# Three chained transformer blocks on one core: causal masks added by VectorE in PSUM, a last tile of squares that goes straight into the means, an activation table fetched early, and branch outputs rounded in two steps

## The reference, cut to what matters

```python
# block 1: three branches are gated and summed, projected, added; then a norm
y  = gates[0]*y_a + gates[1]*y_b + gates[2]*y_c
h  = x + g1 * (y @ w_out)                      # residual "out1"
h2 = modulate(rms_norm(h, norm2_g), sh2, sc2)  # norm "n2", read by the SwiGLU "ff1"
# block 2: two layers of FFN, attention, FFN; the attention has 8 "fox" and
# 4 "diff" heads (each diff head has two score matrices), causal
s = q @ k.T * scale (+ forget bias);  s = where(k_pos <= q_pos, s, -inf)
p = softmax(s)
# between blocks 2 and 3
x = x + 0.5 * swiglu(...)                      # residual "f2_1"
x = _rmsnorm(x, final_norm)                    # row "fin2"
h = rms_norm_3(x, norm_g) * (1 + scale) + shift  # norm "n3"
# block 3: a linear recurrence beside 8 causal attention heads of width 64
```

## Time and profile before

| | us |
|---|---|
| median of three runs | 3472.44 |
| the profiled execution | 3478.79 |
| its span, first to last instruction | 3477.0 |
| TensorE busy in the span | 3398.7 (98%) |
| VectorE, ScalarE, GpSimd busy | 1234.8, 1249.2, 1475.5 |
| mean granted TensorE clock | 0.989 of full |

### The profile page before, as it was taken

The page is one execution under the profiler, slowest core; times in us unless marked ns, Lnnn a source line. Parts: engine busy times, 40 slices in busy tenths (PEclk is TensorE's granted clock), DMA queues, the critical chain, the costliest instruction groups (busy, mean ns, idle before and its releaser), DMA issues.

```text
span 3477.0 us, 38568 instructions
## 1 busy us (share of the span) xinstructions
PE 3398.7 (98%) x15758; PEld 2725.9 (78%) x15758; DVE 1234.8 (36%) x2140; ACT 1249.2 (36%) x1988; POOL 1475.5 (42%) x674
## 2 busy tenths in 40 slices
PE   8999999998999999999999999999999999999998
PEld 5777788887888888887677888888887778888776
DVE  3266775623221134212553111211123642111554
ACT  4534323533222232223554222322233653222543
POOL 4322445654544444445424444444436234444332
PEclk9999999999999999999999999999999999999999
DMA  7211233442333323434213333333333123333211
GB/s 272 67 55 61 97 97 121 157 140 73 122 127 128 98 96 135 139 97 117 67 34 103 97 96 94 94 99 97 94 104 101 39 76 97 97 95 99 73 61 55
DMA packets 102174, 345.41 MB, mean 99 GB/s; under 512 B 12173, under 2 KB 12557, under 8 KB 101838
## 3 DMA queue, kind: packets, MB, share of 16 engines
q1 hardware_dynamic: 101200, 341.10, 30.9%
q10 hardware_dynamic: 798, 1.85, 0.2%
HBM read 336.08 MB, written 2.10 MB: 97 GB/s over the span
## 4 chain that ended last, share of the span: by engine, by line
PE 89%; DVE 4%; ACT 2%; DMA 2%; POOL 1%; issue 1%; SPq 0%; ACTq 0%; DVEq 0%
PE ps L1201 25%; PE ps L1203 24%; PE ps L1202 24%; PE ps L1232 2%; PE ps L1233 2%; PE ps L1234 2%; PE ps L1502 2%; PE ps L1532 1%; DMA t<-in_w_ada 1%; PE ps L1515 1%; POOL t L2675 1%; DVE t L2105 1%; PE ps L1421 1%; PE ps L1435 0%; ACT t L1893 0%
## 5 line engine op out<-in xcount | busy, mean ns | idle before, releaser
L2675 POOL TENSOR_TENSOR t<-t,t 128x1024 fp32r<-128x1024 f32 (+2 forms) x584 | 1354.4, 2321 | 1886.4 <-ACT t L1590 1882.4
L1201 PE MATMUL ps<-t,t 128*128 128x512 f32 x4016 | 1597.8, 398 | 19.6 <-POOL t L2675 13.7
L1203 PE MATMUL ps<-t,t 128*128 128x512 f32 x4016 | 1573.1, 392 | 0.0
L1202 PE MATMUL ps<-t,t 128*128 128x512 f32 x4016 | 1568.4, 391 | 0.0
L1201 PEld LDWEIGHTS ps<-t,t 128*128 128x128 f32 x4016 | 758.0, 189 | 196.0 <-issue 24.1
L1203 PEld LDWEIGHTS ps<-t,t 128*128 128x128 f32 x4016 | 757.4, 189 | 166.1
L1202 PEld LDWEIGHTS ps<-t,t 128*128 128x128 f32 x4016 | 758.3, 189 | 157.7 <-issue 1.7
L1590 ACT CAST t<-t 128x1024 fp32r<-128x1024 f32 (+2 forms) x588 | 584.1, 995 | 575.1 <-PE ps L1203 414.9
L2454 DVE TENSOR_TENSOR t<-t,ps 128x512 f32<-128x512 f32 x110 | 75.7, 688 | 537.0 <-PE ps L1203 522.4
L1656 ACT CAST t<-t 128x512 fp32r<-128x512 f32 x158 | 97.2, 622 | 408.0 <-DVE t L2454 357.5
L1849 ACT ACTIVATE t<-t 128x512 f32<-128x512 f32 x88 | 55.6, 632 | 311.7 <-DVE t L2447 311.6
(11 more groups left out here) (296 smaller groups left out, 2225.3 us busy)
## 6 DMA issues: line engine op xcount, KB each, us to landing
t<-in_w_f1i SPq DMA_DIRECT2D x88, 512.0 KB, 3.6
t<-in_w_f2i SPq DMA_DIRECT2D x88, 512.0 KB, 3.6
t<-in_w_ada SPq DMA_DIRECT2D x72, 512.0 KB, 4.5
t<-in_w_ffi SPq DMA_DIRECT2D x44, 512.0 KB, 4.1
t<-in_w_f1o SPq DMA_DIRECT2D x32, 512.0 KB, 3.5
t<-in_w_f2o SPq DMA_DIRECT2D x32, 512.0 KB, 3.5
t<-in_w_gate SPq DMA_DIRECT2D x24, 512.0 KB, 4.3
t<-in_w_out SPq DMA_DIRECT2D x48, 256.0 KB, 2.7
```

The lines of the kernel that those rows point to most:

```text
L1201: e.matmul(out, wh[:, at], X.hi[c][:, 0:N], start=c == first, stop=False)
L1202: e.matmul(out, wh[:, at], X.lo[c][:, 0:N], start=False, stop=False)
L1203: m = e.matmul(out, wl[:, at], X.hi[c][:, 0:N], start=False, stop=c == final)
L2675: e.tensor_tensor(k.WL[:, n % NHL, 0:w], k.raw[:, j % NRAW, 0:w], f(k.WH[:, n % NHL, 0:w]), ALU.subtract).then_inc(*k.rest.inc(('rest', j) ...
```

## The change

It has four parts.

1. **Masks.** The two mask matmuls of each job go (160 in all). VectorE adds the causal tile, now fp32 in SBUF, to the last 128 columns of both score matrices in PSUM, then takes the two maxima. The two VectorE copies that had prepared the bf16 tiles go too.
2. **Split sums** ("n2" and "n3" only). The sum in SBUF is finished with the seventh tile. The squares of the eighth aren't added by VectorE: TensorE takes the means of the sum, and adds those of the eighth tile's squares in the same PSUM columns.
3. **Table.** Behind the squares of the seventh tile (n = 6) of "out1" and "f2_1" ScalarE takes the square root of a constant into a spare column, and the table of the roots is loaded there, not in front of the real root.
4. **Branches.** `done` is called in steps 7, 8 and 9, with the tiles 0 to 2, 3 to 6, and 7; GpSimd makes the low parts of the tiles 0 and 2 alone, VectorE the others. And in `products`, for "n2", "n3" and "y", the first matmul of an input tile waits for the high part only, the second for the low part.

```diff
     def mixture(i):
-        for j in range(i + 1 if i == 6 else 0):
+        for j in {5: (0, 1, 2), 6: (3, 4, 5, 6), 7: (7,)}[i]:
             on.mixture(YA, j)
-        if i == 7:
-            on.mixture(YA, 7)
...
-        if i >= KT and done is not None:
+        if i >= KT - 1 and done is not None:
             done(i - LEAD)
... (Pool.mixture, low part)
-        if j % 2 == 0:
+        if j in (0, 2):
... (Tensor.products)
+            if X.tag in ('n2', 'n3', 'y'):
+                self.wait_ge('hi', X.tag, c)
+            else:
+                self.wait_ge('lo', X.tag, c)
+            e.matmul(out, wh[:, at], X.hi[c][:, 0:N], start=c == first, stop=False)
             self.wait_ge('lo', X.tag, c)
-            e.matmul(out, wh[:, at], X.hi[c][:, 0:N], start=c == first, stop=False)
             e.matmul(out, wh[:, at], X.lo[c][:, 0:N], start=False, stop=False)
... (Tensor.roots)
-        self.wait_ge('ssq', sq.tag, sq.last)
+        self.wait_ge('ssq', sq.tag, sq.last - sq.split)
         for t in range(sq.n // 128):
-            m = e.matmul(b[:, 2 * t:2 * t + 2], sq.acc[:, t * 128:t * 128 + 128], const(k, 'mean')[:, 0:2], start=True, stop=True)
+            m = e.matmul(b[:, 2 * t:2 * t + 2], sq.acc[:, t * 128:t * 128 + 128], const(k, 'mean')[:, 0:2], start=not sq.split or t == 0, stop=not sq.split, skip_group_check=True)
...
+        self.wait_ge('sq', sq.tag, sq.last)
+        own = sq.slots(k).of(('sq', sq.tag, sq.last))
+        for t in range(sq.n // 128):
+            m = e.matmul(b[:, 2 * t:2 * t + 2], own[:, t * 128:t * 128 + 128], const(k, 'mean')[:, 0:2], start=False, stop=True, skip_group_check=True)
... (Tensor.scores)
-        for (q, kk, ready), b in zip(parts, banks):
-            e.matmul(b[:, 0:n], q[:, qt * 128:n], kk[:, 0:n], start=True, stop=False, skip_group_check=True)
-        self.wait_ge('masks')
-        for c, b in enumerate(banks):
-            m = e.matmul(b[:, qt * 128:n], k.mask[:, 0, :], k.mask[:, 1, :], start=False, stop=True, skip_group_check=True)
+        for c, ((q, kk, ready), b) in enumerate(zip(parts, banks)):
+            m = e.matmul(b[:, 0:n], q[:, qt * 128:n], kk[:, 0:n], start=True, stop=True)
... (Scalar.residual)
+        if n == 6 and (res.sum.split or (res.twin is not None and res.twin.split)):
+            self.root_table()
...
+        e.activation(k.spare, const(k, 'one')[:, 0:1], ACT.Sqrt).then_inc(*k.act.inc())
... (Vector.scores)
+        for key in keys:
+            b = self.bank('s', *key)[:, n - 128:n]
+            self.wait_ge('filled', ('s', *key))
+            e.tensor_tensor(b, b, k.mask, ALU.add).then_inc(*k.dve.inc(('masked scores', key)))
```

More of the change, by code:

```diff
@@ L136 @@
     last = 7
-    bank = False
+    bank = split = False
     def __init__(self, tag, acc, n=S, prior=None, vector=(), first=None, since=()):
@@ L145, in slots, with banked @@
         return ring(k, 'sq ' + self.tag, k.tmp[self.first:], self.since)
-def banked(sq):
-    sq.bank = True
+def banked(sq, split=False):
+    sq.bank, sq.split = (True, split)
     return sq
@@ L201, in memory @@
     k.sm = sbuf(k, [128, 128])
-    k.mask = sbuf(k, [128, 2, 128], BF16)
+    k.spare = sbuf(k, [128, 1])
+    k.mask = sbuf(k, [128, 128])
     k.tmp = [sbuf(k, [128, S]) for _ in range(4)]
@@ L237, in first_memory @@
     k.SIN = place(k, 6, [128, 2, 4, 256])
-    k.CA0 = place(k, 6, [128, 128])
     k.CT = place(k, 30, [128, KT, CTX])
@@ L566, in mixture @@
     def mixture(i):
-        for j in range(i + 1 if i == 6 else 0):
+        for j in {5: (0, 1, 2), 6: (3, 4, 5, 6), 7: (7,)}[i]:
             on.mixture(YA, j)
-        if i == 7:
-            on.mixture(YA, 7)
     branch(on, 1, 'oconv', XA, k.CN, lambda j: ada() if j < 5 else None, done=mixture)
-    res = Residual('out1', lambda j: k.ada[:, 16 + j:17 + j], banked(Sum('n2', k.R[0], S, ('center', 7))), [('ada', 'ada', 2)])
+    res = Residual('out1', lambda j: k.ada[:, 16 + j:17 + j], banked(Sum('n2', k.R[0], S, ('center', 7)), split=True), [('ada', 'ada', 2)])
     for n in range(KT):
@@ L844, in second @@
     if layer:
-        twin = banked(Sum('n3', k.R[2], S, None, range(8)))
+        twin = banked(Sum('n3', k.R[2], S, None, range(8)), split=True)
         twin.slots = nxt.slots
@@ L1266, in roots @@
         self.wait_ge('load', 'con')
-        self.wait_ge('ssq', sq.tag, sq.last)
+        self.wait_ge('ssq', sq.tag, sq.last - sq.split)
         for t in range(sq.n // 128):
-            m = e.matmul(b[:, 2 * t:2 * t + 2], sq.acc[:, t * 128:t * 128 + 128], const(k, 'mean')[:, 0:2], start=True, stop=True)
-        m.then_inc(*k.filled.inc(('filled', ('means', sq.tag))))
+            m = e.matmul(b[:, 2 * t:2 * t + 2], sq.acc[:, t * 128:t * 128 + 128], const(k, 'mean')[:, 0:2], start=not sq.split or t == 0, stop=not sq.split, skip_group_check=True)
+        if not sq.split:
+            m.then_inc(*k.filled.inc(('filled', ('means', sq.tag))))
+            return
+        self.wait_ge('sq', sq.tag, sq.last)
+        own = sq.slots(k).of(('sq', sq.tag, sq.last))
+        for t in range(sq.n // 128):
+            m = e.matmul(b[:, 2 * t:2 * t + 2], own[:, t * 128:t * 128 + 128], const(k, 'mean')[:, 0:2], start=False, stop=True, skip_group_check=True)
+        m.then_inc(*k.filled.inc(('filled', ('means', sq.tag)), ('ssq', sq.tag, sq.last), ('free', ('sq', sq.tag, sq.last))))
     def square(self, sq, t, src, ready):
@@ L1275, in square @@
             self.take(self.k.banks, 'sum', sq.tag, hold=True)
-        if sq.bank and t == sq.last:
+        if sq.bank and t == sq.last - sq.split:
             self.k.banks.let(('sum', sq.tag))
@@ L1598, in begin @@
         e.dma_start(k.AUP, k.t['aup']).then_inc(*load(k, 'aup').inc(('load', 'aup'), by=16))
-        e.dma_start(k.CA0, k.t['con'][:, NCON - 128:NCON]).then_inc(*load(k, 'causal').inc(('load', 'causal'), by=16))
+        e.dma_start(k.mask, k.t['con'][:, NCON - 128:NCON]).then_inc(*load(k, 'causal').inc(('load', 'causal'), by=16))
         self.wait_ge('load', 'cc')
@@ L1838, in residual, with root_table @@
         self.square(res.sum, n, self.k.X[:, n, :], ('x', res.tag, n))
+        if n == 6 and (res.sum.split or (res.twin is not None and res.twin.split)):
+            self.root_table()
+    def root_table(self):
+        k, e = (self.k, self.e)
+        e.activation(k.spare, const(k, 'one')[:, 0:1], ACT.Sqrt).then_inc(*k.act.inc())
     def ffn_gate(self, m, i):
@@ L2056, in square @@
         k, e = (self.k, self.e)
+        if sq.split and t == sq.last:
+            return
         if t and sq.bank:
-            b, end = (self.bank('sum', sq.tag)[:, 0:sq.n], t == sq.last)
+            b, end = (self.bank('sum', sq.tag)[:, 0:sq.n], t == sq.last - sq.split)
             self.wait_ge('sq', sq.tag, t)
@@ L2148, in ctx_keys @@
         k, e = (self.k, self.e)
[L2149 to L2152, removed]
         self.wait_ge('filled', ('kc', tt))
@@ L2395, in mixture @@
     def mixture(self, A, j):
-        if j % 2:
+        if j not in (0, 2):
             self.low(A, j, self.k.O[:, j, :])
@@ L2509, in scores @@
         k, e, n = (self.k, self.e, 128 * qt + 128)
-        for c in range(len(at.parts(h))):
-            key = (at.tag, h, qt, c)
+        keys = [(at.tag, h, qt, c) for c in range(len(at.parts(h)))]
+        self.wait_ge('load', 'causal')
+        for key in keys:
+            b = self.bank('s', *key)[:, n - 128:n]
+            self.wait_ge('filled', ('s', *key))
+            e.tensor_tensor(b, b, k.mask, ALU.add).then_inc(*k.dve.inc(('masked scores', key)))
+        for c, key in enumerate(keys):
             st = self.take(at.stats, 'st', *key)
-            self.wait_ge('filled', ('s', *key))
+            self.wait_ge('masked scores', key)
             e.tensor_reduce(st[:, 0:1], self.bank('s', *key)[:, 0:n], AX, ALU.max).then_inc(*k.dve.inc())
```

## The result

| | before | after |
|---|---|---|
| median, us (10 runs each) | 3472.65 | 3481.9 |
| lowest to highest | 3471.2 to 3479.04 | 3477.79 to 3488.07 |
| profiled execution, us | 3478.79 | 3481.17 |
| its span | 3477.0 | 3479.4 |

The account below looks back on a forecast made before the run. TensorE, busy 98%, was taken to bound the kernel. Masks -4.7, branch end -4.6, "n2" -1.2 and "n3" -0.75 summed to -11.25 us: median 3472.44 to 3461.2, range 3450 to 3468.

Parts of the forecast that it names:

- the sum: Whole kernel: masks -4.7, branch end -4.6, norms -1.2 and -0.75, together -11.25 us; median 3472.44 to 3461.2.
- What bounds the kernel: TensorE, busy 98%: only how closely its instructions follow each other, and the idle 2%, can move the end.
- Masks, what goes: Attention: TensorE's mask matmuls removed, 80 pairs, save 7.3 to 12.8 us; 9 taken.
- Masks, what comes: Attention: VectorE's additions, 0.28 us each, 0.5 a pair, add +3.3 us at existing softmax waits; longer waits +1.
- the four waits that were to grow by 0.5 each: Attention: TensorE waits at 1714.71, 1774.36 and their second-layer twins, four times 0.5, +2.0 us.
- the two that were to grow by 0.25 each: Attention: TensorE waits at 1685.27 and twin 2682.52, additions partly in VectorE's queue, 0.25 each, together +0.5 us.
- Branch end: End of branch 1: TensorE's 5.50 us wait shrinks by 3.2, clock gives 1.4 more, together -4.6 us.
- the rule read from the wait of 2.1 us: Branch end: the remaining wait still leaves about 3.4 us at low clock, 1.6 us lost, clock gain only 1.4.
- "n2": First norm: shorter chain to the root 0.75, first product waiting for the high part only 0.45, together -1.2 us.
- "n3": Later norm: the same shorter chain, -0.75 us; waiting for the high part only brings nothing.
- The chances: Whole kernel: forecast range 0.60, bigger gain 0.15, smaller-gain rivals 0.20, slower 0.05; faster by over 0.2% 0.78.
- a VectorE bound: Attention: each job's softmax chain through VectorE late by 0.5 us, net +24, 3497 us; chance 0.05.

Follow-up runs that it names:

- e7: The kernel before with the masks by VectorE and nothing else changed, every buffer at its address: 3471.38 us, ratio 0.9995.
- e5: The kernel after, spare column put in free space at the end of SBUF, every other buffer at its address of before: 3465.49 us, ratio 0.9977.
- e11: The kernel after, every buffer at its place of before, both norms as before (no split sum, no early table, low part awaited): 3466.77 us, ratio 0.9978.
- e2: The kernel after, with 64 bytes kept for the spare column in place of 32: 3475.76 us, ratio 1.0007.
- e10: The kernel after, every buffer at its place of before, with the branch end as before: 3468.16 us, ratio 0.9979.

## Why the prediction was wrong, point by point

The step that failed is the sum: it has no term for the place of the buffers, which the change moves by 32 bytes. What it left out measured +15.6 us, against a forecast of -11.25 for all the terms it has. The change of instructions was worth 8.5, 13, 17 and 13 us at the four sets of places at which it was measured (d = 64, 96, 128 and 0), so the other terms together were of the right size. In part that is luck, since the masks gave less than their term and the branch end more.

- **What bounds the kernel.** Right: how closely TensorE's instructions follow each other. But I looked at that only around the masks. The diff's `k.spare` and the smaller step from one group to the next in `HH` (680 ns) than in the arena (687) were both to be seen before the run. The missing +15.6 us alone turned -11 into slower.
- **Masks, what goes.** Mis-sized: 9 us taken, about 7.3 measured. From 1640 to 1834 of before, with 3.4 us at half clock in either trace, e7 gains 3.1 us while its three waits on the softmax add up to 5.1 us (5.3 in before: 3.89, 0.98, 0.42). From 2640 to 2830 it gains 0.3, though it waits 0.9 us more and loses up to 1.7 to the clock. Either way the masks gone are worth some 0.09 us a job, 7.3 for 80, which is the lower bound. (From 1590 on e7 gains 4.6, but 1.5 of it is a half-clock stretch ahead of the attention that before has and e7 lacks.)
- **Masks, what comes.** The additions cost 292 ns (0.28 priced), the pair 0.4 to 0.5. Waits grew by 3.7 us, against 4.3 forecast (3.3 + 1), and here the total is luck: the four waits that were to grow by 0.5 each grew by 0.8 to 1.3, 4.3 in all for 2.0, and the two that were to grow by 0.25 each shrank by 3.5 together. 7.3 less 3.7 is 3.6, as the thirteen traces have it, for a forecast of 4.7. Shifts of the clock, which the sum doesn't have here, are as large as this in single executions.
- **Branch end.** The wait went to 1.68 (after) and 1.92 (e5), where 2.3 was worked out. GpSimd's timeline in e5 is the one that was drawn up:

```profile
780.76 1.67 POOL L2717 TENSOR_TENSOR t<-t,t 128x512 f32<-128x512 f32 x1 [2.64 <-DVE t L2334]
782.39 2.57 POOL L2698 TENSOR_TENSOR t<-t,t 128x512 fp32r<-128x512 f32 x2
784.92 2.41 POOL L2692 TENSOR_TENSOR t<-t,t 128x1024 fp32r<-128x1024 f32 x1
787.30 1.74 POOL L2717 TENSOR_TENSOR t<-t,t 128x512 f32<-128x512 f32 x1
790.71 2.35 POOL L2692 TENSOR_TENSOR t<-t,t 128x1024 fp32r<-128x1024 f32 x1 [1.68 <-ACT t L1596]
```

  with ScalarE's cast as what is late next, as forecast (at 789.59, 1.05 us). The clock did not fall behind the shorter wait (1.00 from 794 to 800 in after, with 28 matmuls), so the clock gave 3 us and not 1.4: the rule read from the wait of 2.1 us, that some 3.4 us at half clock would be left, didn't hold for this one. Measured 5.4 to 6, forecast 4.6.
- **"n2".** ScalarE's timeline in e5 (start, us):

```profile
832.30 1.28 ACT L1851 ACT_TABLE_LOAD   x1
...
837.08 0.63 ACT L1629 ACTIVATE t<-t 128x512 f32<-128x512 f32 x1 [2.35 <-DVE t L2421]
838.86 0.27 ACT L1636 ACTIVATE t<-ps,t 128x8 f32<-128x8 f32 x1 [1.14 <-PE ps L1278]
```

  From the last square's start to the root 1.78 us, where before has 2.56 (842.86 to 845.42): 0.78 gained, 0.75 forecast. A load of 1.28 behind the square would have ended at 838.99, 0.13 late, which is all that fetching it early is worth here (0.1 forecast; worked out from these rows, not run by itself). "n2" in all: 1.2 by e5 and e11, 0.4 to 1.2 by all traces, forecast 1.2.
- **"n3".** Right, though the trace of after hides it. There the means stood at half clock: they took 1.80 us, and from the last square (3224.51) to the root (3226.50) it is 1.99, with 2.03 before (3220.11 to 3222.14), where they ran at full clock (1.02). At the same clock the step is seen. ScalarE's timeline of before, then of e5, both at full clock:

```profile
3220.11 0.61 ACT L1623 ACTIVATE t<-t 128x512 f32<-128x512 f32 x1
3220.74 1.28 ACT L1630 ACT_TABLE_LOAD   x1
3222.14 0.27 ACT L1630 ACTIVATE t<-ps,t 128x8 f32<-128x8 f32 x1
...
3206.96 0.61 ACT L1629 ACTIVATE t<-t 128x512 f32<-128x512 f32 x1
3208.20 0.27 ACT L1636 ACTIVATE t<-ps,t 128x8 f32<-128x8 f32 x1 [0.62 <-PE ps L1278]
```

  2.03 us before, 1.24 in e5: 0.79 gained, 0.75 forecast. At half clock it is 2.84 in e11 (3212.94 to 3215.78), which has no split sum there, and 1.99 in after. The expectation of e11, that "n3" gives nothing, compared two clocks. And the load fetched early is worth more here than at "n2": behind the square of e5 it would have ended at 3208.87, 0.67 after the root's start (worked out, not run).
- **The chances.** 0.05 stood for slower, on a VectorE bound. That rival stayed false: the waits grew at the listed places, and by 0.8 us in all behind other divisions (L1515 before, L1511 in e7). The true way to slower was no rival at all.

## What to carry to other kernels

When a diff adds, drops or resizes a buffer, list the addresses of all behind it, and compare the step of the main product's matmuls (start to start) in both traces before any other reading. For fp32r products here, keep moving tiles and weights a multiple of 256 bytes apart; it cost nothing and gave 0.26% to the kernel before. And test parts with every buffer at its old place, or each test measures its layout too. Where a part is worth a few us, compare stretches at the same clock, over several traces: one pair of traces put "n3" at nothing here.

## What the runs showed of the hardware that I had not expected

- Three fp32r matmuls of 128x128 by 128x512 take 680 ns at a distance of 0 by 256 bytes between moving tile and weights, 687 at 64, 697 to 703 at any other multiple of 32, with nothing else running. Where one of the three has d = 64 and the others 0 it is 696, slower than with all three at 64. The length of one in the trace stays at 0.39 to 0.40 us.
- Not one other engine showed it: between before and before with 32 bytes put in, TensorE's busy time grows by 16.1 us, while VectorE's, ScalarE's and GpSimd's change by 2.2, 0.4 and 1.0.
- A table load of 1.28 us with a dependent root straight behind it needs no more than itself: in e5 the load is at 832.30 and its own small root at 833.59.
- Equal waits at one place don't always bring the same clock: behind TensorE's wait of 1.77 to 1.80 us at one place in the second attention two traces (e5, e7) have 3.4 us at half speed and four (after, e2, e10, e11) have none.
